# Four layers of a hybrid decoder on one core: S5 tables moved to VectorE, expert tokens in alternating halves, router and last expert reordered

## The chip, the core and the metric

The kernel runs on one core of a Trainium2 chip. The time is device microseconds of one launch, median of several runs. TensorE (PE in the rows) multiplies, ScalarE (ACT), VectorE (DVE) and GpSimd (POOL) work on tiles in on-chip memory (SBUF) or on the eight accumulator banks (PSUM, `PS`), and SyncE (SP) issues most of the DMA transfers. The engines run side by side and wait for each other by semaphores.

## The reference

256 tokens of width 1024 pass four residual layers. Each has a token mixer and a channel mixer, both behind an RMSNorm:

```python
for i in range(4):
    h = rms_norm(x, norm_mix[i])
    # i = 0, 3: stick-breaking attention; 1: S5 state-space layer; 2: latent attention
    x = x + mixer(h)
    h = rms_norm(x, norm_ffn[i])
    # i = 0, 2: dense SwiGLU, d_ff 2816; i = 1, 3: top-2 of 8 experts, d_ff 1408
    x = x + channel(h)
return rms_norm(x, final_norm)
```

Stick-breaking attention weighs key k of query q by exp(log_sigmoid(z) + sum of log_sigmoid(-z) over the keys between them). The S5 layer is a diagonal complex recurrence: for each of 64 groups of 16 channels 64 complex states, `x_t = a x_{t-1} + b u_t`, output `Re(c x_t)`, then gelu and a gated projection. The expert layer takes `softmax` over the two largest router logits of a token, and adds `gate * (silu(h Wg) * (h Wu)) Wd` of these two experts.

## The kernel before

**Weights.** All matrices are cut into pieces of 128 x 3072 floats (1.5 MB) or less, in the order of use. Each piece goes through the same steps: `load_piece` (L326; SP, into one of four `raw` buffers, when the piece four before has been split), `split_hi` (L336; ScalarE rounds it to `whi`, L344, when TensorE is through with the piece three before), `split_lo` (L346; VectorE subtracts, `wlo`, L351), and TensorE multiplies three times with high and low halves (`split3`, L295, lines L299 to L301). `w_used` counts the pieces used, `lo_done` the pieces split. Each engine's instructions stand in one written order, and its waits are written by hand.

**Stages**, in order: sb0 (attention), dense0, s5, moe0, mla, dense1, sb1, moe1, each behind a norm. A norm (L406 to L488) squares on ScalarE, scales on VectorE, takes the power -0.5 on GpSimd (L456), turns `h` on TensorE (L481), with dummy matmuls (L465) that keep TensorE busy, and splits the turned tokens into `hT_hi` (ScalarE, L427) and `hT_lo` (VectorE, L444).

**Attention** (L540 to L704). For each of eight pairs of heads: scores on TensorE, three functions on ScalarE (`az`), `sp` on VectorE (L690), a triangular select on GpSimd (L704), sums on TensorE (L598 to L600), weights on ScalarE (`pw`, L664), a select, values on TensorE (L615), and the result as `hT_hi` (L668) and `hT_lo` (L695). The projection `proj_dve` (L507) adds three column pieces to `x` (L511) and splits one piece of the next stage in between.

**Dense stage** (L731 to L828). Eight column steps j: gate piece g, turn of the step before (L758, which needs `act`, L819, of VectorE), down piece of two steps before (which needs `alo`, L807), up piece u. VectorE's order in one step is: split, `alo`, split, multiply to `act`, split. In dense0, `s5_powers_dve(j)` (seven instructions, L1083 to L1089) stands before `act` and `s5_taps_dve(j)` (six, L1105 to L1110) behind the last split of each step. They compute for S5 the output taps (`g_out`, left part) and input taps (right part) of table j from `t_bt`, `t_af` and `t_pow`. SP loads `t_bt` and four pieces of `t_af` for table c+1 after it has stored `g_out` of table c, both behind `s5_gd` (one counter of finished tables). The powers `t_pow` and the turn tables `ta_*`, `tb_*` are computed by GpSimd in `s5_tables_pool` (L955) from the start of dense0, many instructions of 32 to 128 columns linked by `glink`; then come eight products for `t_out`, which GpSimd stores, and the pow of norm 2.

**Expert stage** (L1382 on). The router multiplies `h` with the router weights, split as `wrh` (ScalarE, L1513) and `wrl` (VectorE, L1596); VectorE finds the two largest logits, their one-hot `sel` (L1621) and the gates; TensorE adds up counts (L1397, L1398) and ranks of the tokens (L1399 to L1401); VectorE copies these to `route` (L1634 to L1636) and keeps the largest count (L1638, L1640). Then for each of eight experts at most 128 tokens are picked: `pick` (VectorE, L1649), `gather` (TensorE, L1412), a copy `gt` (ScalarE, L1521), `turn_tokens` (L1422), and the turned tokens as `hT_hi` (`ghi`, ScalarE, L1527) and `hT_lo` (`glo`, VectorE, L1697), both in columns 0 to 127 of buffers of 256. An expert has 12 pieces in the order g0 u0 g1 u1 g2 d0 u2 g3 d1 u3 d2 d3; `mact` (L1723) is silu(g) * u, turned to `mhi` (ScalarE, L1560) and `mlo` (VectorE, L1710). The next expert is gathered before g3. `hT_hi` of it is overwritten after u3:

```python
if j == JE - 1 and not last_e:
    used("u", j)
    ghi(e + 1)
sp_("u", j)
```

The results of experts 0 to 6 go through `ysb` (L1576) to memory, and GpSimd fetches each token's rows as `yg` (L1776). VectorE adds them in `add_rows` (L1689), in the last expert: j=0 rows behind the third step's last split, j=1 rows after the last `mact`. The output of expert 7 goes as `yhi`, `ylo` (L1736) through `scatter` (L1432, L1434) and `xadd` (L1659). Experts 1 to 6 are one loop on each engine.

## Time and profile before

| | us |
|---|---|
| median of 3 runs | 1879.08 |
| lowest, highest | 1876.0, 1882.05 |
| the profiled execution | 1886.4 |
| its span, first to last instruction | 1884.8 |
| PE busy | 1772.1 (94%) |
| DVE busy | 1261.0 (67%) |
| ACT busy | 994.2 (53%) |
| POOL busy | 315.8 (17%) |
| mean granted clock of TensorE | 0.975 of 2.4 GHz |
| read from memory | 430.26 MB, 239 GB/s with what is written |

A busy time is the sum of an engine's instructions; matmuls overlap, so a busy TensorE still has small gaps. "Idle before <- X" gives how long an engine stood before an instruction and what released it.

### The profile page before, as it was taken

To read this page: it belongs to the slowest core of one execution; us is meant where nothing else is said; L and a number is where in the kernel's file an instruction comes from. 1 tells how busy PE (TensorE), PEld (TensorE's weight loads), DVE (VectorE), ACT (ScalarE), POOL (GpSimd) and SP (SyncE) were. 2 spreads that over 40 slices of the span, in tenths; PEclk is the share of its full clock that TensorE was granted. 3 is DMA by queue.
4 is the path that set the end of the run, shared out by engine and by line. 5 is a ranking of instruction groups with operands and counts; after the bars stand their busy time and mean duration, and the time that the engine had idled before them with its cause. 6 is when DMAs were issued, how large, how long until landed. Compare 5 with 4: busy or idle time off the path is not lost.

```text
span 1884.8 us, 26446 instructions
## 1 busy us (share of the span) xinstructions
PE 1772.1 (94%) x10809; PEld 1615.1 (86%) x10809; DVE 1261.0 (67%) x1090; ACT 994.2 (53%) x860; POOL 315.8 (17%) x399
## 2 busy tenths in 40 slices
PE   6989999899899999999989999999988999999996
PEld 5978898779788999999878999998976999999995
DVE  4526889674578888888856454435425788888886
ACT  4364333243457777777634343324363667777773
POOL 5825999300000000000200000000020000000011
PEclk9999999999989999999999999999998999999998
DMA  7514786664359998888843045444513689889893
GB/s 296 189 68 168 251 269 235 227 235 156 136 210 352 353 356 346 343 342 342 361 152 135 34 179 178 168 147 166 182 64 112 258 339 360 342 351 357 345 358 144
DMA packets 51877, 452.61 MB, mean 240 GB/s; under 512 B 6432, under 2 KB 6464, under 8 KB 14800
## 3 DMA queue, kind: packets, MB, share of 16 engines
q1 hardware_dynamic: 45888, 430.37, 60.5%
q0 software_dynamic: 5904, 21.02, 3.0%
q8 instruction: 64, 1.05, 0.2%
q14 instruction: 21, 0.17, 0.0%
HBM read 430.26 MB, written 21.10 MB: 239 GB/s over the span
## 4 chain that ended last, share of the span: by engine, by line
PE 73%; DVE 11%; ACT 5%; DMA 4%; issue 4%; POOL 2%; SPq 1%; DVEq 0%; POOLq 0%; ACTq 0%
PE PS L299 20%; PE PS L301 20%; PE PS L300 20%; DVE wlo L351 4%; ACT whi L344 2%; PE PS L1412 2%; DMA yg<-expert_rows,offi 2%; DMA expert_rows<-ysb 1%; DMA t_af<-s_rows_af 1%; PE PS L1422 1%; PE PS L1129 1%; PE PS L1166 1%; PE PS L1456 1%; PE PS L465 1%; DVE h L439 1%
## 5 line engine op out<-in xcount | busy, mean ns | idle before, releaser
L351 DVE TENSOR_TENSOR wlo<-raw,whi 128x3072 fp32r<-128x3072 f32 (+3 forms) x279 | 857.0, 3079 | 313.5 <-ACT whi L344 313.0
L344 ACT ACTIVATE whi<-raw 128x3072 fp32r<-128x3072 f32 (+3 forms) x279 | 708.6, 2541 | 430.8 <-PE PS L301 427.4
L299 PE MATMUL PS<-wlo,hT_hi 128*128 128x384 f32 (+3 forms) x1936 | 633.8, 327 | 10.3 <-DVE alo L807 5.3
L300 PE MATMUL PS<-whi,hT_lo 128*128 128x384 f32 (+3 forms) x1936 | 627.8, 324 | 0.0
L301 PE MATMUL PS<-whi,hT_hi 128*128 128x384 f32 (+3 forms) x1936 | 627.6, 324 | 0.0
L299 PEld LDWEIGHTS PS<-wlo,hT_hi 128*128 128x128 f32 x1936 | 367.6, 190 | 22.5 <-DVE wlo L351 6.9
L300 PEld LDWEIGHTS PS<-whi,hT_lo 128*128 128x128 f32 x1936 | 368.0, 190 | 3.7 <-issue 0.9
L301 PEld LDWEIGHTS PS<-whi,hT_hi 128*128 128x128 f32 x1936 | 367.8, 190 | 0.3
L299 PE MATMUL PS<-wlo,mhi 128*128 128x512 f32 x352 | 146.0, 415 | 10.0 <-DVE mlo L1710 10.0
L300 PE MATMUL PS<-whi,mlo 128*128 128x512 f32 x352 | 140.2, 398 | 0.0
L301 PE MATMUL PS<-whi,mhi 128*128 128x512 f32 x352 | 140.2, 398 | 0.0
L1769 POOL DMA_DIRECT2D expert_rows<-ysb x14 | 7.5, 534 | 759.1 <-ACT ysb L1576 759.1
L299 PEld LDWEIGHTS PS<-wlo,mhi 128*128 128x128 f32 x352 | 66.9, 190 | 28.7 <-issue 10.2
L299 PE MATMUL PS<-hT_lo,whi 128*128 128x256 f32 x288 | 83.2, 289 | 6.9 <-DVE wlo L351 6.9
L456 POOL TENSOR_TENSOR stat<-stat,cst 128x1 f32<-128x1 f32 x18 | 15.0, 838 | 410.9 <-DVE stat L433 405.1
L300 PE MATMUL PS<-hT_hi,wlo 128*128 128x256 f32 x288 | 82.5, 287 | 0.0
L301 PE MATMUL PS<-hT_hi,whi 128*128 128x256 f32 x288 | 82.5, 287 | 0.0
L1549 ACT ACTIVATE msg<-PS 128x384 f32<-128x384 f32 x64 | 29.8, 465 | 97.9 <-PE PS L301 94.8
L301 PEld LDWEIGHTS PS<-whi,mhi 128*128 128x128 f32 x352 | 66.8, 190 | 16.3
L300 PEld LDWEIGHTS PS<-whi,mlo 128*128 128x128 f32 x352 | 67.2, 191 | 12.5
L299 PE MATMUL PS<-wlo,ahi 128*128 128x512 f32 x176 | 71.8, 408 | 0.0
L300 PE MATMUL PS<-whi,alo 128*128 128x512 f32 x176 | 70.4, 400 | 0.0
(355 smaller groups left out, 2092.2 us busy)
## 6 DMA issues: line engine op xcount, KB each, us to landing
raw<-in_weights SPq DMA_DIRECT2D x209, 1536.0 KB, 7.0
raw<-in_weights SPq DMA_DIRECT2D x61, 1024.0 KB, 6.8
raw<-s_tables SPq DMA_DIRECT2D x8, 1536.0 KB, 7.7
s_tables<-g_out SPq DMA_DIRECT2D x8, 1152.0 KB, 6.3
expert_rows<-ysb POOLq DMA_DIRECT2D x14, 512.0 KB, 8.3
t_af<-s_rows_af SPq DMA_DIRECT2D x32, 128.0 KB, 6.2
raw<-in_weights SPq DMA_DIRECT2D x3, 1152.0 KB, 5.4
s_tables<-t_out POOLq DMA_DIRECT2D x8, 384.0 KB, 5.0
```

What stands on the lines that cost most here:

```text
L299: pe.matmul(o, sh, mlw, start=start, stop=False, skip_group_check=True)
L300: pe.matmul(o, sl, mh, start=False, stop=False, skip_group_check=True)
L301: return pe.matmul(o, sh, mh, start=False, stop=stop, skip_group_check=True)
L344: act.activation(whi[p0 % SPL][:, 0:n], raw[p0 % RAW][:, 0:n], ACT.Copy).then_inc(hi_done, 1)
L351: dve.tensor_tensor(wlo[p0 % SPL][:, 0:n], raw[p0 % RAW][:, 0:n], whi[p0 % SPL][:, 0:n].bitcast(F32), ALU.subtract).then_inc(lo_done, 1)
L439: dve.scalar_tensor_tensor(out=h[:, t, :], in0=x[:, t, :], scalar=stat[:, 2, t:t + 1], in1=gain[:], op0=ALU.mult, op1=ALU.mult).then_inc(n ...
L465: pe.matmul(PS[:, bank, :], ident, cst[:, C_IOTA:C_IOTA + 512], start=True, stop=True, skip_group_check=True)
L1129: last = pe.matmul(PS[:, r, 64 * q:64 * q + 64], w[v, 3 - j, q, :], u[v, :, j], start=(j == 0), stop=(j == 3), skip_group_check=True)
L1166: last = pe.matmul(o[:, :, 32 * r:32 * r + 32], xx[:, c % 2, q, r, :], g[:, r, q, 1:5, :], start=(q == 0), stop=(q == 1), skip_group_check ...
L1412: last = pe.matmul(PS[:, 6 + half, :], mo["pick"][:, t, :], hx[:, t, half * 512:half * 512 + 512], start=(t == 0 and i == 0), stop=(t == T ...
L1422: last = pe.transpose(PS[:, 6 + k // 4, (k % 4) * P:(k % 4 + 1) * P], mo["gt"][:, k * P:(k + 1) * P], ident)
L1549: act.activation(mo["msg"][:, 0:w], PS[:, 0, 0:w], ACT.Silu).then_inc(ex.silu, 1)
```

## The change

1. **Powers on VectorE.** A new `s5_turns_dve` does in eight parts, one behind each pair of the first attention from the third on, what GpSimd did at the head of `s5_tables_pool`; GpSimd there waits for the end of the attention, does the first products, then norm 1's pow, then the rest. Powers and taps of table 0 are computed between attention and projection, those of table j+1 in step j of dense0. The inputs of powers and taps are loaded, and the results stored, by separate transfers with their own semaphores (`s5_cn`, `s5_gp`, `s5_gw` and `s5_af`, `s5_gd`, `s5_ww`).
2. **Alternating halves.** Expert e reads columns 0 to 127 of `hT_hi` and `hT_lo` if e is even and 128 to 255 if it is odd, and `ghi` stands before the split of d1's piece without a wait for u3. The loop runs two experts a turn.
3. **Last expert.** `yhi` and `ylo` are made by halves of 512 columns, the scatter goes half by half, `add_rows(0)` stands after the last `mact`, `add_rows(1)` after the last `mlo`.
4. **Router.** `wrh` and `wrl` are made inside the norm, ahead of the turned tokens. TensorE does the ranks first (one matmul for both tiles and one more), then the counts. The gates of `route` and the largest count are computed later.

```diff
+                if a == 0 and i >= 2:
+                    s5_turns_dve(dve, i - 2)
+            if a == 0:
+                s5_taps_dve(dve, 0)
+                proj_dve(dve, b0 + 9, lambda: s5_powers_dve(dve, 0))
...
-                    if f == 0:
-                        s5_powers_dve(dve, j)
+                    if f == 0 and j + 1 < KC:
+                        s5_powers_dve(dve, j + 1)
...
+        def s5_turns_dve(dve, part):
...
+            if part == 0:
+                dve.wait_ge(s5_parE, 1)
+                dve.wait_ge(s5_rd, 32)
+                dve.tensor_tensor(power(1, 0), mag, co, ALU.mult)
+                link(dve.tensor_tensor(power(1, 1), mag, si, ALU.mult))
+                square(power(1, 0), power(1, 1), power(2, 0), power(2, 1))
...
             pool.wait_ge(s5_rd, 32)
+            pool.wait_ge(at_pv, PAIRS)
             load(0)
...
+                if c == 0:
+                    norm_pool(pool, 1)
...
-            dve.wait_ge(s5_af, 80 * (c + 1))
+            dve.wait_ge(s5_gd, c + (c == 0))
+            dve.wait_ge(s5_cn, 16 * (c + 1))
...
+        def s5_powers_load(sp, c):
+
+            if c == 0:
+                sp.wait_ge(at_pv, PAIRS)
+            else:
+                sp.wait_ge(s5_gp, c)
+            sp.dma_start(ff["t_bt"][:, 256:512], s5_bc[c, :, 256:512]).then_inc(s5_cn, 16)
...
+            if n in (3, 7):
+                dve.wait_ge(m_hi, 3 * (n // 4) + 1)
+                dve.tensor_tensor(mo["wrl"][:], mo["wr"][:], mo["wrh"][:].bitcast(F32), ALU.subtract)\
+                    .then_inc(m_lo, 1)
...
+            pe.matmul(PS[:, 5, 0:2 * NE], lower, sel[:].rearrange("p t e -> p (t e)"), start=True, stop=False,
+                      skip_group_check=True)
+            pe.matmul(PS[:, 5, NE:2 * NE], ones, sel[:, 0, :], start=False, stop=True, skip_group_check=True)\
+                .then_inc(m_pe, 1)
             pe.matmul(PS[:, 3, 0:NE], ones, sel[:, 0, :], start=True, stop=False, skip_group_check=True)
             pe.matmul(PS[:, 3, 0:NE], ones, sel[:, 1, :], start=False, stop=True, skip_group_check=True)
...
+                        if j == JE - 1 and not last_e:
+                            ghi(e + 1, 1 - par)
                         if j >= 2:
                             sp_("d", j - 2)
-                        if j == JE - 1 and not last_e:
-                            used("u", j)
-                            ghi(e + 1)
                         sp_("u", j)
...
+            with pe.Fori(1, NE - 2, 2) as e:
+                expert(e, False, False, 1)
+                expert(e + 1, False, False, 0)
...
                     if j == JE - 1:
-                        add_rows(1) if last_e else glo(e + 1)
+                        add_rows(0) if last_e else glo(e + 1, 1 - par)
                         alo(j)
+                        if last_e:
+                            add_rows(1)
                     sp_("u", j)
-                    if j == JE - 2 and last_e:
-                        add_rows(0)
```

## Rows read from the trace of the kernel before

**Rows 1.** Stretches: from:to and length, then PE, PEld, DVE, ACT, POOL busy (instructions), clock, DMA share, GB/s
```profile
162.51:377.93 215.42, 203.16 (x1089) 187.99 (x1090) 172.67 (x148) 72.41 (x44) 174.18 (x218) 0.97 0.70 243
1088.88:1286.19 197.31, 196.79 (x1089) 183.44 (x1090) 90.05 (x44) 72.27 (x44) 0.60 (x1) 1.00 0.49 176
663.00:714.04 51.04, 50.56 (x287) 46.45 (x286) 42.03 (x26) 36.38 (x24) 0.53 (x1) 1.00 0.90 346
501.00:565.00 64.00, 54.28 (x275) 47.70 (x273) 44.26 (x63) 33.95 (x31) 3.14 (x5) 0.84 0.45 160
```

**Rows 2.** TensorE's waits in the whole span: us in total, times, longest
```profile
PE PS L299 <- DVE mlo L1710: 10.0, 16, 3.5
PE PS L758 <- DVE act L819: 7.5, 3, 5.0
PE PS L299 <- DVE alo L807: 5.3, 3, 2.5
```

**Rows 3.** Timeline of TensorE at one seam of experts: start, us, engine, line, operation, idle before
```profile
680.00 0.40 PE L301 MATMUL PS<-whi,mhi 128*128 128x512 f32 x1
680.75 0.47 PE L299 MATMUL PS<-wlo,mhi 128*128 128x512 f32 x1 [0.34 <-DVE mlo L1710]
...
683.38 0.40 PE L301 MATMUL PS<-whi,mhi 128*128 128x512 f32 x1
683.92 0.44 PE L299 MATMUL PS<-wlo,hT_hi 128*128 128x384 f32 x1
```

**Rows 4.** Timeline of ScalarE at the same seam
```profile
676.12 1.09 ACT L1527 ACTIVATE hT_hi<-PS 128x512 fp32r<-128x512 f32 x2 [1.05 <-PE PS L301]
677.09 2.78 ACT L344 ACTIVATE whi<-raw 128x3072 fp32r<-128x3072 f32 x1
```

**Rows 5.** Timeline of VectorE at the same seam
```profile
680.17 0.42 DVE L1710 TENSOR_TENSOR mlo<-PS,mhi 128x256 fp32r<-128x256 f32 x1 [1.25 <-ACT mhi L1560]
680.52 3.35 DVE L351 TENSOR_TENSOR wlo<-raw,whi 128x3072 fp32r<-128x3072 f32 x1
```

**Rows 6.** Timeline of TensorE in the third step of dense0
```profile
221.44 0.45 PE L299 MATMUL PS<-wlo,hT_hi 128*128 128x384 f32 x1 [2.52 <-DVE alo L807]
```

**Rows 7.** Timeline of VectorE in dense0, head and follower of two runs of the powers
```profile
204.17 0.34 DVE L1083 COPY g_out<-t_bt 128x256 f32<-128x256 f32 x1 [5.94 <-DMA t_af<-s_rows_af]
...
208.63 0.96 DVE L819 TENSOR_TENSOR act<-PS,sg 128x768 f32<-128x768 f32 x1
...
255.23 0.48 DVE L1083 COPY g_out<-t_bt 128x256 f32<-128x256 f32 x1
...
262.08 0.96 DVE L819 TENSOR_TENSOR act<-PS,sg 128x768 f32<-128x768 f32 x1
```

**Rows 8.** Timeline of GpSimd in dense0
```profile
166.01 3.55 POOL L979 TENSOR_SCALAR t_pow<-pk 128x32 f32<-128x32 f32 x1
```

**Rows 9.** Timeline of VectorE in the first attention
```profile
111.17 0.96 DVE L690 SCALAR_TENSOR_TENSOR sp<-PS,az 128x768 f32<-128x768 f32 x1 [2.23 <-ACT az L658]
```

**Rows 10.** Chain of work behind sel in moe0's router: start, us, engine, tile, line
```profile
515.99 0.60 PE PS L1397 x2
516.58 0.43 PE PS L1398 x2
...
518.60 0.08 DVE route L1635
...
519.00 0.18 DVE cmx L1638
```

**Rows 11.** Timeline of TensorE at the head of moe1's router
```profile
1438.25 0.28 PE L299 MATMUL PS<-hT_lo,wrh 128*8 128x256 f32 x1 [0.96 <-DVE wrl L1596]
```

**Rows 12.** Timeline of VectorE in moe0's last expert
```profile
925.81 2.48 DVE L1689 SCALAR_TENSOR_TENSOR x<-yg,gy,x 128x1024 f32<-128x1024 f32 x2 [2.52 <-DMA yg<-expert_rows,offi]
...
931.60 0.55 DVE L1710 TENSOR_TENSOR mlo<-PS,mhi 128x384 fp32r<-128x384 f32 x1
...
942.33 1.22 DVE L1736 TENSOR_TENSOR ylo<-PS,yhi 128x1024 fp32r<-128x1024 f32 x1 [1.54 <-ACT yhi L1572]
```

More of the change, by code:

```diff
@@ L505, in proj_pe, with proj_dve @@
                 last.then_inc(w_used, 1)
[L507 removed]
+        def proj_dve(dve, b0, between=None):
             for i, (c0, w) in enumerate(DCOLS):
@@ L515, in proj_dve @@
                     split_lo(dve, b0 + i + SPL)
+                    if between:
+                        between()
         def proj_act(act, b0):
@@ L1208, in s5_act @@
             act.wait_ge(s5_gw, 16 * KC)
+            act.wait_ge(s5_ww, 16 * KC)
             for i in range(KC + 2):
@@ L1427, in scatter @@
             def scatter():
-                pe.wait_ge(ex.ylo, m + 1)
                 for q, bank in enumerate((1, 6, 7, 4)):
-                    t, half = q // 2, q % 2
+                    t, half = q % 2, q // 2
+                    pe.wait_ge(ex.ylo, 2 * m + half + 1)
                     c = slice(half * 512, half * 512 + 512)
@@ L1435, in scatter, with expert @@
                               skip_group_check=True).then_inc(ex.sc, 1)
-            def expert(e, first, last_e):
+            def expert(e, first, last_e, par):
                 g = NE * m + e
@@ L1446, in gate_or_up @@
                         last = split3(pe, PS[:, 0 if kind == "g" else 2, 0:w],
-                                      at((hT_hi, hT_lo), slice(None), k, slice(0, P)),
+                                      at((hT_hi, hT_lo), slice(None), k, slice(par * P, par * P + P)),
                                       at(wp, slice(None), k, slice(None)), k == 0, k == KC - 1)
@@ L1477, in down @@
                                           j == 0 and c == 0, j == JE - 1 and c == kc - 1)
+                        if last_e and j == JE - 1 and half == 0:
+                            last.then_inc(ex.pt, 1)
                     last.then_inc(w_used, 1)
@@ L1526, in ghi, with expert @@
                     act.wait_ge(ex.g, 2 * g + i + 1)
-                    act.activation(hT_hi[:, 4 * i:4 * i + 4, 0:P], PS[:, 6 + i, :].rearrange("p (k s) -> p k s", k=4),
+                    act.activation(hT_hi[:, 4 * i:4 * i + 4, par * P:par * P + P], PS[:, 6 + i, :].rearrange("p (k s) -> p k s", k=4),
                                    ACT.Copy).then_inc(ex.ghi, 1)
-            def expert(e, first, last_e):
+            def expert(e, first, last_e, par):
                 g = NE * m + e
@@ L1579, in moe_act @@
             gathered(0)
-            ghi(0)
-            expert(0, True, False)
-            with act.Fori(1, NE - 1) as e:
-                expert(e, False, False)
-            expert(NE - 1, False, True)
+            ghi(0, 0)
+            expert(0, True, False, 0)
+            with act.Fori(1, NE - 2, 2) as e:
+                expert(e, False, False, 1)
+                expert(e + 1, False, False, 0)
+            expert(NE - 1, False, True, 1)
             rest_act(act, m)
@@ L1734, in expert @@
                 if last_e:
-                    dve.wait_ge(ex.yhi, g + 1)
-                    dve.tensor_tensor(mo["ylo"][:], psf[:, 2048:3072], mo["yhi"][:].bitcast(F32), ALU.subtract)\
-                        .then_inc(ex.ylo, 1)
+                    for half in range(2):
+                        c = slice(half * 512, half * 512 + 512)
+                        if half == 0:
+                            dve.wait_ge(ex.put, 2 * m + 2)
+                        else:
+                            dve.wait_ge(ex.yhi, g + 1)
+                        dve.tensor_tensor(mo["ylo"][:, c], PS[:, 4 + half, :], mo["yhi"][:, c].bitcast(F32), ALU.subtract)\
+                            .then_inc(ex.ylo, 1)
                 else:
@@ L1744, in moe_dve @@
                 split_lo(dve, p0)
-            glo(0)
-            expert(0, True, False)
+            for t in range(TT):
+                i = dve.tensor_tensor(route[:, :, 2, t], oh[:, t, 0, :], oh[:, t, 1, :], ALU.add)
+            link(i)
+            glo(0, 0)
+            link(dve.tensor_reduce(mo["cmx"][:], PS[:, 3, 0:NE], AX.X, ALU.max))
+            dve.tensor_copy(most[:, m:m + 1], mo["cmx"][:]).then_inc(m_ovf, 1)
+            expert(0, True, False, 0)
             where()
-            with dve.Fori(1, NE - 1) as e:
-                expert(e, False, False)
-            expert(NE - 1, False, True)
+            with dve.Fori(1, NE - 2, 2) as e:
+                expert(e, False, False, 1)
+                expert(e + 1, False, False, 0)
+            expert(NE - 1, False, True, 1)
             xadd()
```

225 lines of the change are left out of this document (122 added, 103 removed).

## The prediction

> **What bounds the kernel now.** I read the stretches first, then TensorE's waits, then the timelines of each engine around those waits. TensorE is the bound nearly everywhere: in one turn of the expert loop (51.04 us) it is busy 50.56 us, VectorE 42.03, ScalarE 36.38, and the DMA queues stand at 0.90 and 346 GB/s [rows 1]. So a gain can only come from TensorE's gaps. The two dense stages do the same matmuls, the first beside the state-space tables, the second alone: from the transposes of the norm to the last sum they take 215.42 and 197.31 us, and VectorE's busy time is 172.67 against 90.05 [rows 1]. The difference, 18.1 us, is what the tables cost today. The waits name the places: for act and alo (dense) 7.5 and 5.3 us, for mlo (experts) 10.0 us, its longest 3.5 [rows 2]. Three kinds of gap are thus touched by the change: dense stage 0, the seams between experts, the router and tail of each expert stage.
>
> **Part 1, seams between experts.** Today ScalarE turns the next expert's tokens (hT_hi, 676.12) only once TensorE has left the old ones, and the split of the next expert's first gate piece waits behind it until 677.09 [rows 4]. mhi, mlo (680.17) and wlo (680.52) follow in one chain [rows 5], and TensorE waits for both ends of it: from 680.00 to 680.75, and from 683.38 to 683.92, where the 11 steps between 680.75 and 683.38 take 0.24 each [rows 3]. So 0.51 + 0.30 = 0.81 us are lost at a seam. With halves, hT_hi goes right after mhi of piece 2, where ScalarE is idle, and the chain starts at 676.12, 0.97 us sooner: mlo at 679.20, ready before TensorE's own 680.24; wlo from 679.55 to 682.91, while TensorE would be through at 683.05. What is late next is TensorE itself, by 0.1 us. Both gaps close: 0.81 x 14 seams (seven in each of two layers) = **11.3 us**. Bounds: 5 (only the first gap closes in half of the seams) and 14 (the first matmul after a wait is slower too). Queues: a loop 1.6% faster asks 0.92 of the DMA queues where it has 0.90 [rows 1]; the loads are issued by wlo, which comes sooner too, so I take no cost. The loop runs two experts a turn, so it has two back edges where it had five; their cost is inside the 0.30 us gap at most.
>
> **Part 2, tables in dense stage 0.** Removed from GpSimd and put on VectorE: eight small parts (powers and turn tables, 95 instructions in all) in the attention; the first powers and taps move ahead of the stage, between the attention and its projection; the loads of the powers get their own buffer half and semaphore. Today VectorE stood 5.94 us for a load of t_af before the powers [rows 7], which made TensorE wait for act and then, 2.52 us, for alo at 221.44 [rows 6]. These loads now come one step sooner, so this wait goes, and so does that before the last act, as no table work is left in step 7. What takes its place is GpSimd. Its products ran from about 229 us on; there the powers took 255.23 to 262.08, 6.85 us, against 204.17 to 208.63, 4.46, where GpSimd had only short work [rows 7]. Now GpSimd is at the products from the start of the stage (161 us), so steps 0 to 3 run the slow way. By the order on VectorE: step 0's taps end 3 us later, step 1 has powers 6.5, act 0.9, split 3.4, taps 5.3, split 3.4, so act comes 0.7 us and alo 3.9 us after TensorE wants them. From step 4 (GpSimd through at about 260 us) nothing is late: VectorE's 20.8 us a step lie inside TensorE's 25.7. Left over: 4.8 us, and 1.8 for slow restarts. 18.1 - 6.6 = **11.5 us**. Bounds: 4 (waits as today, 12.3, and only the clock's part back) and 17 (no contention).
> GpSimd's L979, on a tile of 32 columns, took 3.55 us, as long as one wlo of VectorE (3.35, [rows 5]), a split that ran beside it [rows 8]. The Trainium skill (SBUF — State Buffer, the section on its ports) says of this that a VectorE instruction with two SBUF inputs and a GpSimd one exclude each other for a whole instruction, and that the loser fully blocks; the trace agrees. It speaks against this part: selects of the attention, which TensorE waits for, run on GpSimd. By it GpSimd's first table, behind one split and 13 table instructions, would end near 152 instead of 145, still ahead of norm 1; the sum stays, and rival (d) is the rule at its worst.
>
> **Part 3, what that costs the attention.** VectorE idles 2.23 us before every second sp [rows 9], 2.6 before the others. The first part has 18 instructions, the others 6 to 13. Small instructions cost 0.20 us (0.18 and 0.02 of issue) when linked by a semaphore and 0.08 when not [rows 10]. The first has 9 of each: 2.5 us, up to 3.2 as its tiles are 32 wide; the others at most 2.2. So only the first overruns, before an sp with some 2 us of slack. The table loads (six issues on SP's queue behind the last at_pv, near 134 us; some 6 us to landing, by the median of that issue on the page) let taps 0 start near 142.7, after which VectorE has taps 4.4, the x sum 1.1, a split 3.4, powers 4.5 and a sum 1.0 before the last x sum: it starts at 156.95 instead of 156.68. GpSimd's step 0 of the tables now stands ahead of its pow of norm 1, which is wanted at 158.5; it has from 137 on for 8 to 14 us. I take **-0.8 us**; bounds 0 and -4 (loads 3 us later, a slow powers).
> The Trainium skill (VectorE: DVE Perf Modes, The DRAIN you can't avoid) says that a semaphore behind each VectorE instruction costs nothing extra; the rows here disagree, 0.20 against 0.08. By it the first part would be about 1.5 us and this cost 0.
>
> **Part 4, router.** After sel TensorE does five pairs for counts and ranks, 0.60 and four of 0.43 [rows 10], before VectorE may copy. Now two pairs come first, 0.60 + 0.43: 1.29 us sooner. VectorE has just finished its gates then. Behind it two adds (0.08) and a linked reduction and cast (0.20 each) leave the way to pick: 0.5 more. Of this I take **1.7** in each layer. In layer 1 TensorE's logits waited 0.96 us for wrl, which stood behind four hT_lo [rows 11]; wrl is now ahead of them, its load, issued at the head of the norm, should land before ScalarE is through with its held split: **0.9** more. In layer 0 the warm matmuls end no sooner. Together 4.3 (3 to 5).
>
> **Part 5, tail.** add_rows(0) waited for the fetched rows until 925.81 and then ran 2.5 us, with the split and mlo (931.60) of the last but one down piece behind it [rows 12]: this is the 3.5 us of [rows 2]. Moved behind the last act it waits for nothing and mlo comes at about 928.4. But add_rows(1), 2.5 us, and a split of 3.4 now stand between the last mlo and ylo. In layer 0: last mlo 934.0, down piece done 937.3, ylo in halves 940.2 to 941.5, scatter of the first half beside it; before, ylo ran 942.33 to 943.55 [rows 12]. Gain 2.0, and 0.6 as half of the scatter is done: 2.6. Layer 1 has no split behind: 4.5. Together **7.1** (3 to 10).
>
> **Sum.** 11.3 + 11.5 - 0.8 + 4.3 + 7.1 = 33.4 us. The profiled execution took 1886.4 (span 1884.8) and would take 1853.0; the median of the runs is 1879.1, 7.3 lower, so the forecast is 1879.1 - 33.4 = **1846 us**. The smaller and larger ends of the parts together lie at 1868 and 1830; that all fall to one side is unlikely, so the forecast's own range is 1836 to 1857.
>
> **Rivals.**
> (a) Contention eats all of part 2: alo and act are late by as much as before, only elsewhere. For it: 6.85 against 4.46. Against: no load wait is left from step 4 on. Gain 4 instead of 11.5: 1853.
> (b) The seams are only moved: behind the wlo chain stands the next split or a load, and the loop keeps 50.8 us or more. For it: DMA share 0.90 and only 0.1 us of slack. Against: no split in the loop waits for a load. Seams give 3: 1854. That the halves do nothing at all, because hT_hi was not what held wlo, is the end of this case: 1857.
> (c) TensorE's clock. Around the router it averages 0.84 over 64 us [rows 1], so some 20 us (2 x 0.16 x 64) are at the lower of its two levels (1.2 GHz), which costs about 10; with the gap shortened by 1.7 us I allow 8 us of it either way. 1838 or 1854.
> (d) Slower: the lock in the attention. If each small instruction of VectorE waits for half a select (0.38 us) and each select for VectorE, a part lasts 6 to 10 us, 4 to 8 over its idle time, in eight steps with the pow of norm 1 behind: 44 us, less the other 34: 1888. It decides the sign from 4.3 us a step. Against: selects are busy only 3 of 8 us, and VectorE's sp is not stretched beside them.
>
> **Chances.** Forecast 0.52, (a) and (b) and mixtures of them 0.30, (c) 0.10, (d) 0.04; 0.04 for a larger gain than every bound. The range 1834 to 1860 leaves out about 0.17. A measurement here tells 0.3% (5.6 us) from no change: faster 0.93, within 0.04, slower 0.03.
>
> **What will show it.** Seams: the loop's turn 50.2 us and the next hT_hi before the split of piece 11. Dense 0: 204 us from transposes to sum, no wait for t_af, waits for alo at the second and third step. Attention: sp starts at most 1 us later, last x sum within 1 us of 156.7. Router: 1.7 us less from sel to pick. Tail: mlo near 928.4 relative to its gate. Wrong if the turn stays at 51.0, if dense 0 is over 211, or if the attention grows by over 3 us.

## The result, and where the time went

The changed kernel takes 1854.5 us (1851.5 to 1857.8), the kernel before 1878.4 (1876.0 to 1882.1), measured side by side: a ratio of 0.9872, 95% interval 0.9856 to 0.9889. It is 23.9 us faster. The forecast was 1846 us, a gain of 33.4. It gave two ranges, 1836 to 1857 in the sum and 1834 to 1860 in the chances, and the result lies in both. Sign and range held, the gain was some 9 us too large.

The profiled execution of the changed kernel took 1857.8 us, 3.3 above its median. That of the kernel before was some 8 above its own. The two profiles differ by 28.5 us for this reason, the medians by 23.9.

Page of the changed kernel, the engines' busy time:

```profile
span 1856.3 us, 26419 instructions
PE 1759.7 (95%) x10805; PEld 1611.0 (87%) x10805; DVE 1278.6 (69%) x1187; ACT 994.8 (54%) x862; POOL 253.0 (14%) x299
```

The same four stretches as in [rows 1]: dense stage 0, dense stage 1, one turn of the expert loop, the time around the router (from:to and length, PE, PEld, DVE, ACT, POOL busy, clock, DMA share, GB/s):

```profile
164.91:371.20 206.29, 200.02 (x1089) 186.01 (x1090) 161.73 (x135) 72.29 (x44) 103.33 (x102) 0.98 0.72 251
1073.95:1271.30 197.35, 196.79 (x1089) 183.44 (x1090) 90.06 (x44) 72.27 (x44) 0.60 (x1) 1.00 0.49 176
653.87:703.93 50.06, 50.06 (x286) 46.62 (x286) 42.13 (x26) 36.38 (x24) 0.53 (x1) 1.00 0.92 359
494.00:558.00 64.00, 54.90 (x282) 47.39 (x281) 45.93 (x66) 35.04 (x33) 3.15 (x5) 0.89 0.47 171
```

TensorE's waits that answer to [rows 2] (us in total, times, longest):

```profile
PE PS L299 <- DVE alo L832: 4.8, 1, 4.8
...
PE PS L1501 <- DVE ylo L1808: 3.3, 1, 3.3
...
PE PS L299 <- DVE mlo L1777: 2.2, 4, 0.7
PE PS L783 <- DVE act L844: 2.0, 3, 1.0
```

and for ylo, the low half of the last expert's output, in the kernel before:

```profile
PE PS L1432 <- DVE ylo L1736: 4.7, 2, 2.4
```

The seams are gone: a turn is TensorE's own work to the last hundredth, 50.06 of 50.06 us. mlo fell from 10.0 us in 16 waits to 2.2 in 4 (in the three other profiles with the old seams it was 7.3 to 8.2 in 18). Dense stage 0 still stands 8.9 us over dense stage 1, which does the same matmuls; nearly five of them are one wait for alo. The wait for ylo was there before, 2.4 us in the last expert of each layer. It is gone in layer 1 and has grown to 3.3 us in layer 0.

The table sets the starts of the same events of each profile against each other: the stretches run from the transposes of one norm to those of the next, or from one gather of tokens (0 to 7 in each layer) to the next. The gain is that of the one pair of profiles; the last column says what the experiments below make of it.

| stretch | before | after | gain | what it is |
|---|---|---|---|---|
| start to norm 1 (attention 0) | 160.8 | 163.2 | -2.4 | turns 1.5, rest mostly clock |
| norm 1 to norm 2 (dense stage 0) | 222.1 | 213.0 | 9.1 | tables |
| norm 2 to norm 3 (S5) | 121.9 | 124.0 | -2.1 | clock |
| norm 3 to gather 1, layer 0 | 55.6 | 52.8 | 2.8 | router |
| gather 1 to gather 7, layer 0 | 306.6 | 301.3 | 5.3 | seams |
| gather 7 to norm 4 | 85.2 | 83.0 | 2.2 | one seam, and a late row fetch only in this profile; the tail lost 1 |
| norm 4 to norm 7 | 481.1 | 481.1 | 0.0 | untouched |
| norm 7 to gather 1, layer 1 | 55.4 | 52.4 | 3.0 | router |
| gather 1 to gather 7, layer 1 | 306.6 | 301.3 | 5.3 | seams |
| gather 7 to the end | 89.6 | 84.2 | 5.4 | one seam, and the tail |

### The profile page after: what moved, and what is told of

Same layout as the page of the kernel before. It is cut to its first block and busy times, and to the rows that moved or that the text cites. A ratio compares the mean times of both kernels' runs of the same rounds, so it can differ in the third digit from the quotient of the medians.

```text
span 1856.3 us, 26419 instructions
## 1 busy us (share of the span) xinstructions
PE 1759.7 (95%) x10805; PEld 1611.0 (87%) x10805; DVE 1278.6 (69%) x1187; ACT 994.8 (54%) x862; POOL 253.0 (14%) x299
## 5 line engine op out<-in xcount | busy, mean ns | idle before, releaser
L300 PE MATMUL PS<-hT_hi,wlo 128*128 128x256 f32 x288 | 82.3, 286 | 0.0
L301 PE MATMUL PS<-whi,ahi 128*128 128x512 f32 x176 | 69.7, 396 | 0.0
```

What stands on the lines that cost most here:

```text
L300: pe.matmul(o, sl, mh, start=False, stop=False, skip_group_check=True)
L301: return pe.matmul(o, sh, mh, start=False, stop=stop, skip_group_check=True)
```

## The parts one by one

The change was taken apart into four kernels, each the kernel before with one part alone.

**Seams alone**

```
- k, slice(0, P)                      # TensorE's token operand
+ k, slice(par * P, par * P + P)
- with pe.Fori(1, NE - 1) as e:
-     expert(e, False, False)
+ with pe.Fori(1, NE - 2, 2) as e:
+     expert(e, False, False, 1)
+     expert(e + 1, False, False, 0)
...
+ if j == JE - 1 and not last_e:
+     ghi(e + 1, 1 - par)
  if j >= 2:
      sp_("d", j - 2)
- if j == JE - 1 and not last_e:
-     used("u", j)
-     ghi(e + 1)
```

> The kernel before with only the alternating halves (and the loop of two experts a turn, hT_hi's copies ahead of the split of down piece 11). Theory A, the seam is what the profile of after shows, 51.04 us a turn to 50.06: 14 seams of 0.98, so 13.7 us less than before, about 0.7%. Rival B, as predicted beforehand: 14 x 0.81 = 11.3 us less. Rival C, part of it is given back where the loop ends, since the last expert keeps its old order and its row fetch was what ended last there: 10 us less or under. In the profile: a turn of two experts takes 100.1 us (A), and the stretches ahead of the first expert stand as in the kernel before.

Ratio 0.9933 (0.9912 to 0.9955), so 12.6 us less (8.5 to 16.5). The gathers stand 50.07 us apart where they stood 51.04. From gather 1 to gather 2, across the first seam, it is 50.94 for 51.39, only 0.46 less. So 12 seams of 0.97 and two of 0.46 make 12.6. The interval of the times holds theory A (13.7) and rival B (11.3) alike; the turns decide for A, with a smaller first seam. The loop of two experts is part of this kernel too, so fewer back edges could be a cause beside the halves. The turns speak against it: every second one of the new kernel has a back edge in it and the others have none, and they differ by at most 0.07 us (50.12 and 50.05).

**Tables alone**

```
+ if a == 0 and i >= 2:
+     s5_turns_dve(dve, i - 2)
- proj_dve(dve, b0 + 9)
+ if a == 0:
+     s5_taps_dve(dve, 0)
+     proj_dve(dve, b0 + 9, lambda: s5_powers_dve(dve, 0))
...
- if f == 0:
-     s5_powers_dve(dve, j)
+ if f == 0 and j + 1 < KC:
+     s5_powers_dve(dve, j + 1)
```

> The kernel before with only the S5 tables moved (first table and turns on VectorE in attention 0, the rest of dense stage 0; two semaphores of the router are merged to have room, which moves nothing). Theory A: dense stage 0 shorter by 9.1 us, attention 0 longer by 1.5 (the 18 instructions of the first part), S5 as before: 7.6 us less. Rival B: the 2.4 us in attention 0 and the 2.1 us in S5 of the profile of after belong to the tables too: 9.1 - 2.4 - 2.1 = 4.6 us less. Rival C, the prediction: 11.5 - 0 + 0.8 = 12.3 us less. In the profile: a wait for alo of about 4.8 us in dense stage 0, and S5 with norm 3 as long as before (121.9 us) by A, 124 by B.

Ratio 0.9960 (0.9946 to 0.9974), so 7.5 us less (4.9 to 10.2). Dense stage 0 with its norm took 213.1 us, as in the changed kernel; in the kernels without the tables it took 222.1, 221.8, 224.6, 220.5 and 220.3. The wait for alo was 4.77 us to the hundredth. S5 took 124.0. By this one profile theory B would be right, by the times theory A; the runs further down decide it.

**Router alone**

```
+ pe.matmul(PS[:, 5, 0:2 * NE], lower, sel[:].rearrange("p t e -> p (t e)"), start=True, stop=False, ...)
+ pe.matmul(PS[:, 5, NE:2 * NE], ones, sel[:, 0, :], start=False, stop=True, ...).then_inc(m_pe, 1)
  pe.matmul(PS[:, 3, 0:NE], ones, sel[:, 0, :], start=True, stop=False, ...)
  pe.matmul(PS[:, 3, 0:NE], ones, sel[:, 1, :], start=False, stop=True, ...)
- pe.matmul(PS[:, 5, 0:NE], lower, sel[:, 0, :], ...)
- pe.matmul(PS[:, 5, NE:2 * NE], ones, sel[:, 0, :], ...)
- pe.matmul(PS[:, 5, NE:2 * NE], lower, sel[:, 1, :], ...)
```

> The kernel before with only the router's change (weights split in the norm, ranks ahead of counts, the sums of the gates behind pick). Theory A, the prediction: 2 x 1.7 + 0.9 = 4.3 us less. Rival B, the ledger of the two profiles: 2.1 + 2.6 = 4.7 less. Rival C: the shorter pause changes nothing of TensorE's clock there but the pick is later held by the queue for the gathered rows, so under 2.5 us.

Ratio 0.9995 (0.9980 to 1.0010): 0.9 us less (3.8 less to 1.9 more). Its profile shows the part at work all the same: from the norm's transposes to the first gather 13.1 us in layer 0, where five kernels with the old router took 14.6 to 15.5, and 12.3 in layer 1, where they took 13.9 to 15.0. Either the time is given back elsewhere or the measurement is off. The part was measured again by taking it out of the changed kernel (below).

**Tail alone**

```
- add_rows(1) if last_e else glo(e + 1)
+ add_rows(0) if last_e else glo(e + 1)
  alo(j)
+ if last_e:
+     add_rows(1)
  sp_("u", j)
- if j == JE - 2 and last_e:
-     add_rows(0)
...
+ for half in range(2):
+     dve.tensor_tensor(mo["ylo"][:, c], PS[:, 4 + half, :], mo["yhi"][:, c].bitcast(F32), ALU.subtract)...
```

> The kernel before with only the last expert's change (fetched rows added behind the last act, output split and scattered by halves). Theory A, the ledger of the two profiles with one seam of 0.98 taken off each layer: 1.2 in layer 0 and 4.4 in layer 1, 5.6 us less. Rival B, the prediction: 2.6 + 4.5 = 7.1 less. Rival C: in layer 0 the second add of rows and the split of 3.4 us now stand ahead of the output's split and give back all: 4.4 less in all, layer 0 nothing.

Ratio 0.9976 (0.9961 to 0.9992): 4.5 us less (1.5 to 7.3). The profile says less. From gather 7 to norm 4 the tail alone took 83.2 us, and two kernels with the old tail and the old seams took 82.3: layer 0 lost 0.9. In layer 1, from gather 7 to the end, it took 85.5 where those two took 87.1 and 88.6, a gain of 1.6 to 3.1. The waits say the same: two waits for ylo of 2.4 us have become one of 3.3 in layer 0 and none in layer 1. So rival C is nearest, and layer 0 is worse than nothing. The reason stands in two timelines of VectorE. First the kernel with the router alone, whose tail is the old one: the row added is not waited for.

```profile
922.90 2.28 DVE L351 TENSOR_TENSOR wlo<-raw,whi 128x2048 fp32r<-128x2048 f32 x1
925.10 2.48 DVE L1686 SCALAR_TENSOR_TENSOR x<-yg,gy,x 128x1024 f32<-128x1024 f32 x2
```

In the profile of the kernel before, this add had stood idle for the fetched rows, 2.52 us in layer 0 [rows 12] and 1.09 in layer 1:

```profile
1852.58 2.48 DVE L1689 SCALAR_TENSOR_TENSOR x<-yg,gy,x 128x1024 f32<-128x1024 f32 x2 [1.09 <-DMA yg<-expert_rows,offi]
```

In five other profiles that have the add in its old place (among them the last kernel below) VectorE stood idle before it in none of layer 0 and in one of layer 1 (0.75). The forecast had priced a late row fetch that the other profiles do not show. Second, the changed kernel:

```profile
920.61 0.42 DVE L1777 TENSOR_TENSOR mlo<-PS,mhi 128x256 fp32r<-128x256 f32 x1
920.96 2.47 DVE L1755 SCALAR_TENSOR_TENSOR x<-yg,gy,x 128x1024 f32<-128x1024 f32 x2
923.46 3.36 DVE L351 TENSOR_TENSOR wlo<-raw,whi 128x3072 fp32r<-128x3072 f32 x1
926.74 1.28 DVE L1808 TENSOR_TENSOR ylo<-PS,yhi 128x512 fp32r<-128x512 f32 x2
```

yhi's halves were there at 923.5 and 924.9, but the second add and a split stand ahead of ylo: this is the new wait of 3.3 us.

Together the four parts measured alone make 25.5 us, and the whole change 23.9. Each of these figures is uncertain by some 3 to 4 us, so they agree, but an overlap of a few us between parts would not be seen.

## What holds each part

**Where the hT_hi copy stands**

```
  if j >= 2:
      sp_("d", j - 2)
+ if j == JE - 1 and not last_e:
+     ghi(e + 1, 1 - par)       # behind the split again, without used("u", j)
  sp_("u", j)
```

> As e1_seams (the kernel before with the alternating halves and the loop of two), but ScalarE copies the next tokens to hT_hi behind the split of down piece 11, where it stood before, only without its wait for the last up piece. Theory A, what held the seam was the place behind the split (2.8 us) as much as the wait: the turn is 50.5 to 51.0 us, so 6 us less than before at most. Rival B, only the wait counted: the turn is 50.07 as in e1_seams, 12.6 us less than before.

Ratio 0.9926 (0.9905 to 0.9947), the turn 50.07 us: rival B. In ScalarE's timeline the copy follows the split, and the next split still starts ahead of time:

```profile
670.24 1.92 ACT L344 ACTIVATE whi<-raw 128x2048 fp32r<-128x2048 f32 x1 [1.92 <-PE PS L301]
672.07 1.07 ACT L1528 ACTIVATE hT_hi<-PS 128x512 fp32r<-128x512 f32 x2
673.11 2.78 ACT L344 ACTIVATE whi<-raw 128x3072 fp32r<-128x3072 f32 x1
```

So the second buffer half, which takes ScalarE's wait for the old tokens away, is all of this part. The new place in the order is worth nothing.

**The contention in dense stage 0**

```
  if c == 0:
      norm_pool(pool, 1)
+     pool.wait_ge(s5_gd, 3)
```

> The kernel after, with GpSimd's products of tables 1 to 7 held back until VectorE is through with the taps of table 2 (near 220 us). Theory A, contention: in the changed kernel the powers and taps of steps 0 to 2 of dense stage 0 take 6.9, 6.3, 5.3 and 6.5 us beside the products; alone they take 4.5, so the waits of TensorE for act (0.99) and alo (4.77) go and with them the half clock behind the long one: dense stage 0 falls from 213.1 to about 206 us from transposes to transposes. Rival B, order: VectorE is late there by its own work (split, powers, act, split, taps, split), contention or not: 212 or more. Rival C: the stall only moves to where the products now run (steps 3 to 6, or S5's first table): 211 to 213, with the wait at another step. Against the kernel before: A 0.9835, B and C 0.987.

Ratio 0.9867 (0.9839 to 0.9894), dense stage 0 at 210.8 us from transposes to transposes. TensorE's waits over 0.6 us in the stage:

```profile
246.85 0.44 PE L299 MATMUL PS<-wlo,hT_hi 128*128 128x384 f32 x1 [2.12 <-DVE alo L832]
...
301.40 0.69 PE L299 MATMUL PS<-wlo,hT_hi 128*128 128x384 f32 x1 [2.72 <-DVE alo L832]
```

The wait at 225 us is gone, so it did come of GpSimd's work (theory A for its cause), and 4.84 us of waits have come up where the products now run (rival C, at the lower edge of its 211 to 213). GpSimd working without a pause makes VectorE late wherever it stands. That leads to the next kernel.

**One table a step**

```
  for c in range(KC):
+     if c >= 1:
+         pool.wait_ge(s5_gd, c + 1)
```

> The kernel after, with GpSimd making one table a step of dense stage 0: table c waits for the taps of c on VectorE. Theory A: a step has 4.9 us of VectorE's time to spare (25.7 - 20.8); a table beside it takes about half the step and lengthens VectorE's work by 2 to 3 us, so no step is late: no wait for alo, dense stage 0 at 206 to 207.5 us from transposes to transposes where it was 213.1 (after) and 210.8 (products held back, then run on end). Rival B: the first steps are late by VectorE's own order and the wait comes back whatever GpSimd does: over 210. Rival C: the last tables come too late for S5 and its start waits: the gain of the stage comes back in S5 (122 us as it is).

Ratio 0.9841 (0.9827 to 0.9854), 1845.6 us. Dense stage 0 took 204.2 us from transposes to transposes, better than theory A. Its matmuls, and S5 behind it:

```profile
164.24:361.70 197.46, 196.94 (x1089) 183.33 (x1090) 149.59 (x135) 72.31 (x44) 84.27 (x102) 1.00 0.75 262
```

```profile
366.71:488.58 121.87, 114.73 (x1229) 104.00 (x1229) 70.24 (x108) 45.80 (x84) 6.30 (x12) 0.97 0.49 178
```

197.46 us is what dense stage 1 takes without any table work (197.35): the tables now cost TensorE nothing, and the clock stayed up through the stage. VectorE was busy for 149.6 us where it was for 161.7 with the same 135 instructions. The 12 us between went into longer instructions; as only GpSimd's pace was changed, they are read as time spent waiting for it inside them. The powers of one table show it: in the changed kernel

```profile
182.88 0.72 DVE L1132 COPY g_out<-t_bt 128x256 f32<-128x256 f32 x1
...
189.73 0.95 DVE L844 TENSOR_TENSOR act<-PS,sg 128x768 f32<-128x768 f32 x1
```

and with one table a step

```profile
182.19 0.29 DVE L1134 COPY g_out<-t_bt 128x256 f32<-128x256 f32 x1
...
186.38 0.95 DVE L844 TENSOR_TENSOR act<-PS,sg 128x768 f32<-128x768 f32 x1
```

6.85 us against 4.19 for the same seven instructions.

**The turns in attention 0**

```
- if a == 0 and i >= 2:
-     s5_turns_dve(dve, i - 2)
+ if a == 0 and 1 <= i < 9:
+     s5_turns_dve(dve, i - 1)
```

> The kernel after, with each part of the turns one step of the attention sooner, so that the first part (18 instructions, 3.85 us) falls into VectorE's idle 5.6 us behind the second sp. Theory A: the 1.54 us by which the fourth sp was late go, and nothing else moves: the steps from sp 2 to sp 7 take 20.1 to 20.3 us instead of 21.7. Rival B: what made it late is the lock with GpSimd's selects, and sp 2 is now late instead: 21.7 again. Against the kernel before: A 0.9865, B 0.987, too near for the times; the sp rows decide.

Ratio 0.9872 (0.9846 to 0.9897). In the changed kernel the first part of the turns runs from 109.57 and the fourth sp comes at 113.42, 5.16 us behind the third:

```profile
108.26 0.96 DVE L709 SCALAR_TENSOR_TENSOR sp<-PS,az 128x768 f32<-128x768 f32 x1 [5.60 <-ACT az L677]
109.23 0.42 DVE L714 TENSOR_TENSOR hT_lo<-PS,hT_hi 128x256 fp32r<-128x256 f32 x1
109.57 0.20 DVE L1009 TENSOR_TENSOR t_pow<-s_par 128x32 f32<-128x32 f32 x1
...
113.42 0.96 DVE L709 SCALAR_TENSOR_TENSOR sp<-PS,az 128x768 f32<-128x768 f32 x1
```

One step sooner the part ends at 106.4, the third sp still waits 2.08 us for ScalarE, and the fourth comes at 112.35, 3.88 us behind it:

```profile
108.47 0.96 DVE L709 SCALAR_TENSOR_TENSOR sp<-PS,az 128x768 f32<-128x768 f32 x1 [2.08 <-ACT az L677]
...
112.35 0.96 DVE L709 SCALAR_TENSOR_TENSOR sp<-PS,az 128x768 f32<-128x768 f32 x1
```

From sp 2 to sp 7 (the third to the eighth) it is 20.5 us for 21.7: 1.2 of the 1.54 at once, and from norm 0 to norm 1 149.8 for 151.3. Theory A, though its 20.1 to 20.3 us were not reached: without the tables these steps took 20.0. The times don't show the part, as was expected: 0.9872 is the changed kernel's own ratio.

The other 0.5 us are the seven other parts. In the changed kernel they leave VectorE no slack: the longest idle time before an sp from the fourth on is

```profile
121.67 0.96 DVE L709 SCALAR_TENSOR_TENSOR sp<-PS,az 128x768 f32<-128x768 f32 x1 [0.32 <-DVE pk L1004]
```

where it had been 2.2 to 2.6 us in every step.

**The split ahead of ylo**

```
- sp_("u", j)
+ if j < JE - 1 or not last_e:
+     sp_("u", j)
...
  dve.sem_inc(x_up, 1)
+ split_lo(dve, moe_split(m, NE - 1, NX["u", JE - 1])[0] + SPL)
```

> The kernel after, with the split that stood between the last mlo and ylo in the last expert of layer 0 (3.4 us) moved behind the x sum of the scatter. Theory A, this split is what ate the tail's gain in layer 0: ylo starts right behind its yhi, 3.1 us sooner, and the next norm's transposes about 2.5 us sooner (from the eighth gather 80.5 instead of 83.0). Rival B: the held split is then late for the norm's end and the first projection of attention 1, and the 2.5 us come back there. Layer 1 has no such split and stays. Against the kernel before: A 0.986, B 0.987.

Ratio 0.9886 (0.9862 to 0.9910): no gain by the times.

```profile
919.70 2.47 DVE L1755 SCALAR_TENSOR_TENSOR x<-yg,gy,x 128x1024 f32<-128x1024 f32 x2
922.33 0.69 DVE L1809 TENSOR_TENSOR ylo<-PS,yhi 128x512 fp32r<-128x512 f32 x1 [0.17 <-ACT yhi L1641]
...
928.90 3.36 DVE L351 TENSOR_TENSOR wlo<-raw,whi 128x3072 fp32r<-128x3072 f32 x1 [1.74 <-issue]
```

ylo did come right behind its yhi and the scatter 3.0 us sooner, as theory A says; but the split, moved into the norm, gave half of it back there: from gather 7 to norm 4 81.5 us for 83.0, a gain of 1.5 where 2.5 was expected. Attention 1 took 136.0 for 135.0 with more of the lower clock. Theory and rival are both partly right.

**The router again, taken out**

```
- pe.matmul(PS[:, 5, 0:2 * NE], lower, sel[:].rearrange("p t e -> p (t e)"), ...)
+ pe.matmul(PS[:, 5, 0:NE], lower, sel[:, 0, :], ...)      # and the counts ahead of it again
```

> The kernel after with the router's part undone (weights split behind the norm, counts ahead of ranks, the gates' sums ahead of pick); the merged semaphores stay. Theory A, the profiles: from the norm's transposes to the first gather 1.6 us more in layer 0 and 2.0 in layer 1, so 3.6 to 4.2 us more than after. Rival B, the first measurement by the times, the router is worth 0.9 us (3.8 to -1.9): 1 us more than after, with the rest given back where the clock is low behind the shorter pause.

> The kernel after itself, unchanged, beside the others on the same chip. Every theory: 0.987 of the kernel before. What it tells: S5 took 124.0 us in the first profile of after and 120.8 to 121.9 in three variants of it; if the 2 us were the tables' they are here again, if they were the clock's chance S5 is at 122.

The changed kernel beside it: 0.9888 (0.9873 to 0.9903), 1855.3 us. Without the router's part 0.9907 (0.9891 to 0.9923). By the two ratios the router is worth 0.0019 of the time, 3.6 us, by the two medians (1857.5 and 1855.3) 2.2, and by the first measurement 0.9. Each has some 3 us of uncertainty or more, so the times alone do not tell it from nothing. From norm 3 to the first gather it took 15.5 us for 13.5, from norm 7 14.9 for 12.3. In layer 1 the wait for wrl [rows 11] is back without the part and gone with it. The profiles decide. From norm 3 to the second gather the six with the old router took 55.0 to 55.6 us and the eight with the new one 52.8 to 54.2; from norm 7 it was 53.8 to 55.4 and 52.3 to 52.8. The means differ by 2.1 us each time, 4.2 together. Some of it is TensorE's clock: in the first of these stretches it was at the lower level for 17.1 to 20.5 us with the old router and 13.0 to 17.1 with the new one.

The unchanged kernel's second profile answers the question of S5. It was 124.0 us again:

```profile
375.91:499.92 124.01, 118.22 (x1228) 106.08 (x1229) 70.33 (x108) 45.79 (x84) 6.30 (x12) 0.94 0.48 175
```

but two kernels that are the changed kernel up to the end of S5, with the split moved in the last expert and with the old router:

```profile
376.27:498.11 121.84, 114.69 (x1228) 103.95 (x1228) 70.25 (x108) 45.84 (x84) 6.30 (x12) 0.97 0.49 178
```

```profile
375.04:495.38 120.34, 113.19 (x1229) 102.44 (x1229) 70.24 (x108) 45.79 (x84) 6.30 (x12) 0.99 0.50 180
```

The other engines' busy times are the same; the column that differs is the granted clock, 0.94, 0.97 and 0.99. So the 2.1 us of S5 are the clock's and not a cost of the tables' work. The kernel with the router alone, which has no tables in its attention, took 123.5 us for the same stage with 10.9 us at the lower clock. That the stages before S5 make the low clock likelier with the tables of the changed kernel is not excluded: it was 0.94 in three profiles of five.

**All three repairs**

```
+ if c >= 1:
+     pool.wait_ge(s5_gd, c + 1)          # one table a step
...
+ if a == 0 and 1 <= i < 9:
+     s5_turns_dve(dve, i - 1)            # turns one step sooner
...
- add_rows(0) if last_e else glo(e + 1, 1 - par)
+ add_rows(1) if last_e else glo(e + 1, 1 - par)
  alo(j)
- if last_e:
-     add_rows(1)
  sp_("u", j)
+ if j == JE - 2 and last_e:
+     add_rows(0)
```

> The kernel after with three edits: tables one a step (as e9_paced), each part of the turns a step sooner (as e6_turns_sooner), and the fetched rows added where the kernel before added them (behind the last but one up piece, and ahead of the last mlo), the output still in halves. Theory A: 5.6 to 6.5 us (dense stage 0) + 1.5 (attention 0) + 2.4 (layer 0's output split 2.4 us sooner) = about 10 us less than after, 0.994 of it. Rival B, the row fetch is late as in the profiled run of the kernel before, and layer 0's part is nothing or a loss: 7 us less. Rival C, the clock's low stretches take up what the waits gave: under 5 us less.

Ratio 0.9809 (0.9795 to 0.9822), 1840.0 us (1838.7 to 1841.7): 15.3 us faster than the changed kernel on the same chip, 35.6 faster than the kernel before, and more than theory A's 10. Between the two profiles 8.8 lie in dense stage 0, 1.9 ahead of norm 1, 3.1 from gather 7 to norm 4; 2.1 in S5 and 2.8 in attention 1 are the clock's, and 1.4 around the first router go the other way. So some 13.8 us are the repairs' by the stretches that they touch.

```profile
909.74 3.35 DVE L351 TENSOR_TENSOR wlo<-raw,whi 128x3072 fp32r<-128x3072 f32 x1
913.01 1.35 DVE L1810 TENSOR_TENSOR ylo<-PS,yhi 128x512 fp32r<-128x512 f32 x2
```

With the second add ahead of the last mlo again, ylo comes 3.6 us behind mlo (909.40) where it was 6.1; the rows had been fetched in time in both layers. This profile also takes the tail's two halves apart. With the output in halves and the adds in their old place the stretch from gather 7 is 80.0 us in layer 0 and 84.3 in layer 1. The two kernels with the new seams and the whole old tail took 81.5 and 82.3 in layer 0 and 86.3 and 86.1 in layer 1, so the halves are worth about 2 us a layer (in layer 0 a part may be the clock, which did not fall there in this profile). The moved adds make it 83.1 and 84.2: 3.1 us lost in layer 0, 2.5 of them in the wait for ylo (3.3 for 0.7), and nothing won in layer 1.

## The prediction, step by step

**Seams: 11.3 predicted, 12.6 measured. Right in mechanism, 1.3 too small.** The two gaps closed as described. The 0.81 us were the gaps that the rows show between matmuls; a turn lost 0.97. The rest stands right behind the two gaps, in the first matmul after each. In the kernel before:

```profile
681.05 0.40 PE L300 MATMUL PS<-whi,mlo 128*128 128x512 f32 x1
681.28 0.40 PE L301 MATMUL PS<-whi,mhi 128*128 128x512 f32 x1
...
684.20 0.34 PE L300 MATMUL PS<-whi,hT_lo 128*128 128x384 f32 x1
684.37 0.34 PE L301 MATMUL PS<-whi,hT_hi 128*128 128x384 f32 x1
```

From the matmul at 680.75 [rows 3] to the next it is 0.30 us, from that to the following 0.23; from the one at 683.92 it is 0.28, then 0.17. These 0.07 and 0.11 us are the missing 0.16 to within 0.02, and the prediction had named them only as the reason of its upper bound. That its chain starts 0.97 us sooner is a chance agreement: the new turn is bound by TensorE's own 50.06 us and not by that chain. Working against it, the first seam of each layer gave only 0.46, which the prediction did not see. Expert 1 has the row addresses to work out on VectorE, and its mact is late in both kernels; as its other wait went, this one grew from 0.23 to 0.63:

```profile
582.61 3.36 DVE L351 TENSOR_TENSOR wlo<-raw,whi 128x3072 fp32r<-128x3072 f32 x1
585.89 0.55 DVE L1790 TENSOR_TENSOR mact<-PS,msg 128x384 f32<-128x384 f32 x1
```

The chain that the halves replaced now stands so, ScalarE's copy right behind mhi and 8 us ahead of the last mlo, at 670.30:

```profile
662.33 1.09 ACT L1597 ACTIVATE hT_hi<-PS 128x512 fp32r<-128x512 f32 x2
```

Of the reasons given, "goes right after mhi of piece 2" is the one that does nothing; "once TensorE has left the old ones" is the whole of it. The DMA queues' share went to 0.92 as foreseen, and rival (b), seams only moved, is out.

**Tables in dense stage 0: 11.5 predicted, 9.1 measured.** The working came near the waits: act late by 0.7 and alo by 3.9 were forecast (4.6, which the sum took as 4.8), 0.99 and 4.77 came. Of the waits for alo that it wanted at the second and third step only the one at the third is there. Nothing was late from step 4 on but the last act, by 0.52 us where it had been 4.99; dense stage 1 has the same 0.52, so this is no table work. Of the 2.4 us between forecast and measurement 1.0 are these waits (5.8 for 4.8). The other 1.4 are in TensorE's own busy time, 200.02 us for 196.79 in dense stage 1, so 3.2 where 1.8 had been allowed without a row. Behind the long wait the changed kernel had 6.8 us at the lower clock; with the wait gone there was none, and the busy time was 196.94. Rival (a), gain 4, fell short of what came. What the prediction did not ask is whether the contention had to be there: it took GpSimd's pace as given, and this was worth 9.7 us (1855.3 to 1845.6), as much as the whole part gave. That pace was set by the change itself: in the kernel before, the products ran only from 228 us on.

**Attention 0: 0.8 us of cost predicted, about 1.5 to 1.7 measured, with the reason misplaced.** "So only the first overruns, before an sp with some 2 us of slack" is right in kind. The size failed: 18 instructions were priced at 2.5 to 3.2 us and took 3.85 (109.57 to 113.42). Linked ones took 0.22 to 0.26 and unlinked ones 0.11 to 0.14 on these tiles, and some of the first five were longer still (up to 0.48 from one start to the next) while GpSimd's selects ran; the rows used were from the router's tiles of eight columns. The delay of the last x sum behind the taps, by contrast, which was priced at 0.27, is not there: from sp 7 to the last x sum it is 29.5 us in both. The bound of 4 us held. The 2.2 us for the other parts were low as well: the second part, of 12 instructions, took 2.6 us (109.73 to 112.35 with the turns one step sooner), and parts two to eight together cost 0.1 to 0.5 us. Of the 2.4 us between the two profiles the rest is a step ahead of the first part, which took 6.6 us instead of 5.0 at the lower clock; it did so in two of the five kernels without the tables too.

The Trainium skill (VectorE: DVE Perf Modes, The DRAIN you can't avoid) has a semaphore behind each VectorE instruction cost nothing. The rows of the changed kernel disagree again, 0.22 to 0.26 against 0.10 to 0.14 us from start to start on 32 columns.

**Router: 4.3 predicted, 4.2 by fourteen profiles, 0.9 to 3.6 by the times.** From sel to pick, the chain of [rows 10], it was 3.71 us (515.76 to 519.47) and is 2.04:

```profile
510.97 0.18 DVE L1691 TENSOR_TENSOR sel<-oh 128x16 f32<-128x16 f32 x1
...
513.01 0.60 DVE L1715 TENSOR_SCALAR pick<-cst,cur 128x128 fp32r<-128x128 f32 x2
```

1.67 us, as the 1.7 predicted, and the wait for wrl of 0.96 is gone. By the profiles the term was right; the times cannot see it clearly.

**Tail: 7.1 predicted, 1 to 2 by the profiles, 4.5 (1.5 to 7.3) by the times. This step failed.** "add_rows(0) waited for the fetched rows until 925.81 ... this is the 3.5 us of [rows 2]" took a late fetch of one execution for the kernel's habit. In the others that wait does not exist (but for 0.75 us once), so moving the add gains nothing, and what the move costs, 2.5 us of add and a split of 3.4 between the last mlo and ylo, was seen (ylo at 940.2) but set against a gain that was not there. Layer 0 lost 1 us where 2.6 had been forecast, layer 1 won 2 for 4.5. What was won came of the output in halves, about 2 us a layer; the sum had counted 0.6 for it in layer 0 and gave no working for layer 1.

**The base.** The sum of 33.4 was built on the profile that was 8 us above its median and then taken off the median. Of those 8 us some 4 lie in the two tails (76.6 and 75.2 us from the last gather to the scatter, where two kernels with the same tail took 73.7 and 73.5 to 74.3), and a part of them was in the sum. To subtract stalls that only this execution had from a median that already lies below it counts them twice. By the terms, the tail was 5 to 6 us too large, the tables 2.4, the attention's cost 0.8 too small, the seams 1.3 too small and the router about right: 7 to 8 of the 9 us. The rest is within the error of the times. The lower end of the sum's outer bounds, 1830, should be 1833 by its own parts (14 + 17 + 0 + 5 + 10 = 46); nothing hangs on it.

**Rivals.** (c), the clock, moved single stretches by 2 to 5 us in both directions, in stages that no part touches as well; only around the router and behind the long waits did it follow the change. (d), the lock in the attention, did lengthen single small instructions beside a select (up to 0.48 us), but the whole cost is 1.5 to 1.7 us where 44 were feared. The first part overran by 1.5 and the others by next to nothing, though they used up all of VectorE's slack.

## What to carry to other kernels

A wait read from one profiled execution is a term only if it repeats. Above all a wait for a DMA that depends on timing should be looked for in a second profile, or priced at zero on one side of the range, and an execution well above its median says that some of its waits are its own. Background work on GpSimd is to be paced by the engine that it disturbs: the same eight tables cost TensorE 8.9 us in one go and nothing one to a step. When a step is moved in an in-order queue, count what is then ahead of the next thing on the path, against a gain that is certain.

## What the runs showed of the hardware

GpSimd and VectorE hold each other up, in both directions. With one table a step, a GpSimd subtraction that takes 0.74 us elsewhere took 3.74 beside one VectorE split. It ended 0.60 us after the split, so it seems to have waited for the whole of it:

```profile
195.26 0.61 POOL L1063 TENSOR_TENSOR t_tmp<-ta_s,tb_s 128x256 f32<-128x256 f32 x1
195.96 3.74 POOL L1064 TENSOR_TENSOR t_out<-t_out,t_tmp 128x256 f32<-128x256 f32 x1
```

```profile
195.56 3.54 DVE L351 TENSOR_TENSOR wlo<-raw,whi 128x3072 fp32r<-128x3072 f32 x1 [0.98 <-ACT whi L344]
```

In the other direction a split took 4.70 us instead of 3.36 with the products held back, and instructions of the powers 1.0 to 1.2 us instead of 0.69. The Trainium skill (SBUF — State Buffer, Summary: rules for kernel authors) advises to schedule whichever of the two is off the critical path. The runs agree that one is held up by the other, but that GpSimd's work was off the path did not help by itself: VectorE's was not, and only spreading GpSimd's made room.

TensorE's granted clock fell in stretches that differ from run to run and from kernel to kernel. The same S5 stage took 120.3, 121.8 and 124.0 us at a mean clock of 0.99, 0.97 and 0.94, and the stretch of attention 1, which no version changes, 130.4 us with none of it at the lower clock and 136.0 with 12.3 us. One profile's difference of 2 to 5 us in a stage says nothing about a change unless another engine's rows move with it.
